# Expert outputs weighted at the PSUM eviction and accumulated into the residual in DRAM by the scatter

## What is computed

```
h2 = rmsnorm(x, g_ffn)
# top-1 of 4 groups, then top-2 of the 8 experts in it: 2 weights per token
for g in range(N_GROUPS):
    a = einsum('td,edf->tef', t, w_gate[g]); u = einsum('td,edf->tef', t, w_up[g])
    hid = silu(a) * u * combine[:, g, :, None]
    out = out + einsum('tef,efd->td', hid, w_down[g])
x = x + out
gate = sigmoid(rmsnorm(x, g_ple) @ w_ple_gate)
x = x + gate * (p @ w_ple_proj)
return rmsnorm(x, g_final)
```

## Time and profile before

| | us |
|---|---|
| median of 3 runs | 1550.75 (1549.37 to 1552.88) |
| the profiled execution | 1552.96 |
| its span on the slowest core, core 0 | 1551.4 |
| spans of the other seven cores | 1510.9 to 1547.7 |
| PE busy | 1103.8 (71%) |
| DVE busy | 733.3 (47%) |
| ACT busy | 727.7 (47%) |
| POOL busy | 491.0 (32%) |

### The profile page before, as it was taken

One profiled execution on the slowest core, in us unless ns is written; L12 is line 12 of the kernel. 1 busy time (PEld: TensorE's weight loads), 2 busy tenths in 40 slices (PEclk: granted clock), 3 DMA queues, 4 the chain that ended last, 5 costly groups with the idle time before them and its releaser, 6 DMA issues.

```text
span 1551.4 us, 24781 instructions; the slowest of 8 cores (1510.9 to 1551.4 us)
## 1 busy us (share of the span) xinstructions
PE 1103.8 (71%) x7772; PEld 716.7 (46%) x7772; DVE 733.3 (47%) x1283; ACT 727.7 (47%) x1376; POOL 491.0 (32%) x576
## 2 busy tenths in 40 slices
PE   2456389724972598870597999988989896852882
PEld 1123145413541354450475776766767674530341
DVE  4899877534752388437421222211212221116983
ACT  4888977625662488620142333332333332313652
POOL 3231132311221133130333433433434353111673
PEclk9767669856985598775698999999999998885986
DMA  9999995997699769935197898998788899568422
GB/s 224 217 142 136 110 106 89 139 135 102 84 136 136 107 90 132 167 129 189 29 237 180 214 219 208 220 241 226 185 227 200 224 162 167 148 214 306 163 109 110
DMA packets 74560, 254.32 MB, mean 164 GB/s; under 512 B 23735, under 2 KB 30647, under 8 KB 56000
## 3 DMA queue, kind: packets, MB, share of 16 engines
q0 software_dynamic: 43984, 134.60, 56.7%
q1 hardware_dynamic: 30448, 118.13, 23.0%
HBM read 434.85 MB, written 120.59 MB: 358 GB/s over the span
## 4 chain that ended last, share of the span: by engine, by line
PE 36%; DMA 26%; issue 12%; DVE 11%; ACT 6%; POOL 4%; another core or an unknown queue 4%; SPq 1%; DVEq 0%; ACTq 0%; POOLq 0%
PE ps L1377 14%; DMA sb_R<-h2scr,sb_R 7%; DMA sb_R<-xin 7%; PE ps L1349 7%; DMA xscr<-sb_R 3%; DMA sb_R<-w_pp 3%; PE ps L966 3%; DMA h2scr<-sb_R 2%; PE ps L1332 2%; PE ps L750 2%; DMA sb_R<-yscr 1%; DVE sb_R L1483 1%; POOL sb_R L1524 1%; PE ps L1003 1%
## 5 line engine op out<-in xcount | busy, mean ns | idle before, releaser
L1377 PE MATMUL ps<-sb_R 128*128 128x256 bf16 x3008 | 347.6, 277 | 6.2 <-DMA sb_R<-wall,sb_R 4.7
L1377 PEld LDWEIGHTS ps<-sb_R 128*128 128x128 bf16 x3008 | 298.7, 99 | 56.2 <-issue 7.1
L1382 DVE TENSOR_TENSOR sb_R<-sb_R,ps 128x512 bf16<-128x512 f32 x94 | 64.6, 688 | 317.7 <-PE ps L1377 269.1
L1359 POOL DMA_INDIRECT yscr<-sb_R x94 | 94.6, 1007 | 337.7 <-DVE sb_R L1356 296.8
L1349 PE MATMUL ps<-sb_R 128*128 128x512 bf16 x752 | 178.2, 390 | 0.8
L1381 ACT ACTIVATE sb_R<-ps 128x512 f32<-128x512 f32 x94 | 56.1, 597 | 258.1 <-PE ps L1377 209.5
L1335 ACT COPY sb_R<-ps 128x1024 bf16<-128x1024 bf16 x94 | 95.2, 1012 | 133.7 <-PE ps L1332 130.0
L1356 DVE COPY sb_R<-ps 128x512 f32<-128x512 f32 x94 | 64.9, 691 | 175.6 <-ACT sb_R L1354 89.7
L1303 POOL DMA_INDIRECT sb_R<-h2scr,sb_R x94 | 97.4, 1036 | 91.0 <-DVE sb_R L1262 62.2
L1349 PEld LDWEIGHTS ps<-sb_R 128*128 128x128 bf16 x752 | 73.0, 100 | 85.7 <-issue 13.9
L840 PE MATMUL ps<-sb_R 128*128 128x512 bf16 x128 | 36.3, 434 | 72.9 <-ACT sb_R L996 71.0
(11 more groups left out here) (248 smaller groups left out, 2098.1 us busy)
## 6 DMA issues: line engine op xcount, KB each, us to landing
wbf<-wall POOLq DMA_DIRECT2D x48, 1024.0 KB, 52.8
sb_R<-wbf SPq DMA_DIRECT2D x48, 1024.0 KB, 13.9
sb_R<-wall POOLq DMA_DIRECT2D x48, 1024.0 KB, 17.0
...
```

Of the source, the lines that this page charges most:

```text
L1359: return e.indirect_dma_start(y_d, bass.IndirectOffsetOnAxis(ap=didx[:, blk:blk + 1], axis=0), y.ap, None, bounds_check=breg(e, 2 * T_OWN ...
L1377: ins = e.matmul(pv[:, q * N:(q + 1) * N], lhsT=w_[:, c, f * P:(f + 1) * P], rhs=hT_[:, c, 0:N], start=(c == 0), stop=(c == 7))
```

## The change

Each expert output is scaled by its token's routing weight when it is evicted from PSUM, and the scatter adds it to the token's row of `xscr`, the residual, in DRAM. `yscr`, its loads in the tail and the two DVE operations per tile are gone. The one-hot matmuls now bring per slot the token number (from a new constant table `tokv`) and the weight `wsl`; the index of the second output place is not needed. These one-hot tiles are f32 instead of bf16.

Since two scatters may add to the same row, each scatter is given waits: with n scatters recorded before it and h the half of its block pair, `after=Yd[max(0, n - 2 - h):]`, which always includes the one just before. The first one also waits for all writes of `xscr`. In the tail the loads of x now wait for all scatters.

```diff
+ACC_FROM = lambda n, h: max(0, n - 2 - h)
...
-    y_d = dt("yscr", [2 * T_OWN, D], F32, kind="Internal").ap()
...
+        OHr = [a.rearrange("p t e -> p (t e)").rearrange("p (j n) -> p j n", j=4) for a in (gef, Ssl)]
+        OHq = [R.alloc(8 * NB).rearrange("p (j n) -> p j n", j=4) for _ in range(2)]
...
-            S.op("dve", lambda e, z=z: e.tensor_scalar(OHq[z][:, :, 0:NB], OHm[z], pc1, None, ALU.mult),
+            S.op("dve", lambda e, z=z, lo=lo: e.tensor_tensor(OHq[z][:, :, 0:NB], OHm[z], bg(tokv[:, lo:lo + 4], NB), ALU.mult),
                  reads=[OHm_b[z], cst_b], writes=[OH_b[z]])
-            S.op("dve", lambda e, z=z, lo=lo: e.tensor_tensor(OHq[z][:, :, NB:2 * NB], OHm[z], bg(iota[:, lo:lo + 4], NB), ALU.mult),
+            S.op("dve", lambda e, z=z, lo=lo: e.tensor_tensor(OHq[z][:, :, NB:2 * NB], OHm[z], bg(w12[:, lo:lo + 4], NB), ALU.mult),
...
-        dv(lambda e: e.tensor_copy(iT, p5[:, NB:2 * NB]), extra=[p5])
...
-        dv(lambda e: e.tensor_copy(iTi, iT))
-        dv(lambda e: e.tensor_scalar(iTi, iTi, 1, None, ALU.arith_shift_right))
-        dv(lambda e: e.tensor_copy(dsf, iTi))
-        dv(lambda e: e.scalar_tensor_tensor(dsf, dsf, float(P), inv, ALU.mult, ALU.add))
-        S.op("dve", lambda e: e.tensor_copy(gidx, dsf), reads=[rtb], writes=[ix_b])
-        dv(lambda e: e.scalar_tensor_tensor(dsf, iT, float(P), inv, ALU.mult, ALU.add))
-        S.op("dve", lambda e: e.tensor_copy(didx, dsf), reads=[rtb, ix_b], writes=[ix_b])
+        S.op("dve", lambda e: e.tensor_copy(gidx, inv), reads=[rtb], writes=[ix_b])
+        S.op("dve", lambda e: e.tensor_copy(wsl, p5[:, NB:2 * NB]), reads=[p5], writes=[ws_b])
...
-                        S.op("act", lambda e, y=y, pd=pd: e.copy(y[:, 0:512], pd.ap), reads=[pd], writes=[y])
+                        S.op("act", lambda e, y=y, pd=pd, blk=blk: e.activation(y[:, 0:512], pd.ap, AF.Copy, scale=wsl[:, blk:blk + 1]),
+                             reads=[pd, ws_b], writes=[y])
                     else:
-                        S.op("dve", lambda e, y=y, pd=pd: e.tensor_copy(y[:, 512:1024], pd.ap), reads=[pd], writes=[y])
+                        S.op("dve", lambda e, y=y, pd=pd, blk=blk: e.tensor_scalar(y[:, 512:1024], pd.ap, wsl[:, blk:blk + 1], None, ALU.mult),
+                             reads=[pd, ws_b], writes=[y])
...
-                    return e.indirect_dma_start(y_d, bass.IndirectOffsetOnAxis(ap=didx[:, blk:blk + 1], axis=0),
-                                                y.ap, None, bounds_check=breg(e, 2 * T_OWN - 1), oob_is_err=False)
+                    return e.indirect_dma_start(xs_d, bass.IndirectOffsetOnAxis(ap=gidx[:, blk:blk + 1], axis=0),
+                                                y.ap, None, bounds_check=breg(e, T_OWN - 1), oob_is_err=False, compute_op=ALU.add)
                 yb = B(f"Yd{blk}")
+                S.dmaop("pool", fn, reads=[y, ix_b] + (Xd if not Yd else []), writes=[yb], sembuf=y, after=Yd[ACC_FROM(len(Yd), h):], kb=512)
                 Yd.append(yb)
-                S.dmaop("pool", fn, reads=[y, ix_b], writes=[yb], sembuf=y, kb=512)
...
-                S.dmaop("sp", lambda e, x=x, ot=ot: e.dma_start(out=x.ap, in_=xs_d[ot * P:(ot + 1) * P, :]), reads=[Xd[ot]], writes=[x], kb=512)
-                S.dmaop("sp", lambda e, yt=yt, ot=ot: e.dma_start(out=yt.ap.rearrange("p (k d) -> p k d", k=2),
-                                                                 in_=y_d[ot * 2 * P:(ot + 1) * 2 * P, :].rearrange("(k p) d -> p k d", k=2)),
-                        reads=Yd, writes=[yt], kb=1024)
-                for k, wk in ((0, w1), (1, w2)):
-                    S.op("dve", lambda e, ot=ot, k=k, wk=wk, yt=yt, x=x: e.scalar_tensor_tensor(
-                        x.ap, yt[:, k * D:(k + 1) * D], wk[:, ot:ot + 1], x.ap, ALU.mult, ALU.add),
-                        reads=[yt, cw_b, x], writes=[x])
+                S.dmaop("sp", lambda e, x=x, ot=ot: e.dma_start(out=x.ap, in_=xs_d[ot * P:(ot + 1) * P, :]), reads=[Xd[ot]] + Yd, writes=[x], kb=512)
```

More of the change, by code:

```diff
@@ L589, in build @@
     wall_d = dt("wall", [NE, P, 12288], F32, kind="ExternalInput").ap()
-    cst_d = dt("cst", [P, 2 * P + 1], F32, kind="ExternalInput").ap()
+    cst_d = dt("cst", [P, 2 * P + 33], F32, kind="ExternalInput").ap()
     wbf_d = dt("wbf", [NE, P, 12288], BF16, kind="Internal").ap()
@@ L632, in build @@
         ix_b = B("ix"); ox_b = B("ox"); cw_b = B("cw"); cst_b = B("cst")
-        gidx = R.alloc(NB, I32, ix_b); didx = R.alloc(NB, I32, ix_b); oidx = R.alloc(NOVF, I32, ox_b)
-        w1 = R.alloc(NT, F32, cw_b); w2 = R.alloc(NT, F32, cw_b)
-        cst = R.alloc(2 * P + 1, F32, cst_b)
+        gidx = R.alloc(NB, I32, ix_b); ws_b = B("ws"); wsl = R.alloc(NB, F32, ws_b); oidx = R.alloc(NOVF, I32, ox_b)
+        w12 = R.alloc(2 * NT, F32, cw_b); w1 = w12.rearrange("p (t k) -> p t k", k=2)[:, :, 0]; w2 = w12.rearrange("p (t k) -> p t k", k=2)[:, :, 1]
+        cst = R.alloc(2 * P + 33, F32, cst_b)
+        tokv = cst[:, 2 * P + 1:2 * P + 33]
         iota = cst[:, 0:P]; utri32 = cst[:, P:2 * P]; pc1 = cst[:, 2 * P:2 * P + 1]
@@ L1136, in build @@
         slots3 = slots.rearrange("p (t k) -> p t k", t=NT)
-        OHr = [R.alloc(4 * P, BF16).rearrange("p (j n) -> p j n", j=4) for _ in range(2)]
-        OHq = [R.alloc(8 * NB, BF16).rearrange("p (j n) -> p j n", j=4) for _ in range(2)]
+        OHr = [a.rearrange("p t e -> p (t e)").rearrange("p (j n) -> p j n", j=4) for a in (gef, Ssl)]
+        OHq = [R.alloc(8 * NB).rearrange("p (j n) -> p j n", j=4) for _ in range(2)]
         OHm1 = R.alloc(4 * NB).rearrange("p (j n) -> p j n", j=4); OHm = [OHm1, OHm1]; OHm1_b = B("OHm"); OHm_b = [OHm1_b, OHm1_b]
         OH_b = [B(f"OH{i}") for i in range(4)]; OHr_b = [B(f"OHr{i}") for i in range(4)]
-        p1T = R.alloc(NB); iT = R.alloc(NB); inv = R.alloc(NB); dsf = R.alloc(NB); iTi = R.alloc(NB, I32)
+        p1T = R.alloc(NB); inv = R.alloc(NB)
         rtb.ranges.append((disp_off, R.off)); rtb.older = None
@@ L1238, in build @@
                  reads=[qr_b, cst_b], writes=[OHm_b[z]])
[L1239 removed]
+            S.op("dve", lambda e, z=z, lo=lo: e.tensor_tensor(OHq[z][:, :, 0:NB], OHm[z], bg(tokv[:, lo:lo + 4], NB), ALU.mult),
                  reads=[OHm_b[z], cst_b], writes=[OH_b[z]])
[L1241 to L1242 removed]
+            S.op("dve", lambda e, z=z, lo=lo: e.tensor_tensor(OHq[z][:, :, NB:2 * NB], OHm[z], bg(w12[:, lo:lo + 4], NB), ALU.mult),
+                 reads=[OHm_b[z], cw_b], writes=[OH_b[z]])
             def mmi(e, g=g, z=z):
@@ L1440, in build @@
         R.off = off0
-        TY = R.pool(S, "ty", 2048, 3)
         tx_off = R.off; R.off += 10240
@@ L1551, in make_in_maps @@
     cst = np.ascontiguousarray(np.concatenate([np.broadcast_to(ar[None, :], (P, P)),
-                                               (ar[:, None] < ar[None, :]).astype(np.float32), ar[:, None] + 1.0], axis=1))
+                                               (ar[:, None] < ar[None, :]).astype(np.float32), ar[:, None] + 1.0,
+                                               (np.arange(2 * NT) // 2 * P).astype(np.float32)[None, :] + ar[:, None] + 1.0], axis=1))
     w_pg = f(inp["w_ple_gate"])[0]; w_pp = f(inp["w_ple_proj"])[0]
```

3 lines of the change are left out of this document (1 added, 2 removed).

## The result

| | before | after |
|---|---|---|
| median, us | 1551.82 (1549.37 to 1555.83) | 1786.68 (1767.6 to 1806.21) |
| the profiled execution | 1552.96 | 1779.88 |
| its span on the slowest core | 1551.4 (core 0) | 1778.3 (core 1) |
| DVE busy | 733.3 | 691.5 |
| PE busy | 1103.8 | 1152.4 |

The change makes the kernel slower: a ratio of 1.147, with a 95% interval of 1.1361 to 1.1578. It saves what it removes, 17 MB of traffic and 42 us of DVE, and loses 227 us of span. The forecast was 1733 us with a range of 1635 to 1875. Some executions are slowed on one half of the chip; medians and ranges are over all executions, ratios and their intervals over the undisturbed ones alone, so a ratio can differ from that of two medians.

A forecast was written before the change was run, and what follows sets the result against it. PE bounds the kernel; the waits would put POOL's chain of landings ahead of it. Rounds +165, start +10, end +40, dispatch +4, tail -37 sum to +182 on 1553: 1735 profiled, 1733 us median, range 1635 to 1875.

The forecast's parts named there:

- The landing behind wall loads: Expert rounds: the even expert's first scatter lands behind wall loads and overflow gathers, 31.5 us after the first wall load.
- rival 1: Expert stage: POOL's slack absorbs the waits, leaving tail and dispatch, 1520 us; needs landings behind wall loads under 14; chance 0.09.
- The near-empty scatter: Second halves and overflow blocks: one landing, issue to semaphore, takes 3.1 us, bounds 2.2 and 3.75.
- The full one: Full accumulating scatter: one landing takes 5.4 us, the data time doubled for the add; bounds 4.2 and 8.5.
- Rival 2: Expert stage: the add itself is slow, a full scatter costs 8 us more, twice a round, 1940 us; chance 0.09.
- The 1.5 us set aside for sharing: Expert rounds: SP's three loads share the engines with wall loads, 1.5 us a round (0 to 7), making it 53.
- Start of the stage: Start of the expert stage: the first scatters stand behind two wall loads, +10 us (5 to 15).
- End of the stage: Last wall loads: transfers run dry while POOL walks scatters and gathers between sets, four gaps of 10, +40 us (20 to 70).
- The evictions: Expert stage: evictions by weight on ACT and DVE cost the same as before and are hidden anyway.
- The dispatch: Just ahead of the expert stage: fewer DVE operations, -2.5, and f32 one-hot matmuls, +6.5; together +4 us (-2 to +40).
- The tail: After the last scatter: yscr loads and DVE adds gone, xscr loads wait for the last scatter; -37 us (-22 to -57).
- 3, half absorbed: Expert stage: PE loses only half of the 15 us a round, 1651 us; counted inside the forecast's range, at its low end.

The follow-up runs named there:

- e1: The kernel before with only the waits added, each plain scatter to yscr waiting for the one just before: 1709.67 us, ratio 1.0986.
- e2: The kernel after, waits kept, its scatter overwriting instead of adding, so the residual and one of a token's two outputs are lost: 1687.27 us, ratio 1.0843.

## Why the prediction was right

**What bounds the kernel.** Right: PE before, POOL's chain of landings after, with PE waiting for what POOL issues late. Three of the signs that were named came, the second a little short: the scatter's own transfer as main releaser, with 348.0 us (over 300 was said); single waits of up to 25.9 us behind each set of wall loads (25 to 32 was said); sets 55.5 us apart (50 to 56). The idle time of PE in the stage rose by 198.6 us, where about 200 were said: PE was busy 565.5 of 650 us from 750 to 1400 before and 616.9 of 900 from 750 to 1650 after, 84.5 us idle against 283.1. It was to rise at the transposes alone; of the 220 us that PE now waits for POOL's late transfers, 78 are at the weights of overflow experts, which the prediction didn't name.

**The landing behind wall loads** was the step with most weight, read from a near-empty gather in the earlier trace rows: 31.5 us after the first load, measured 32.0 with its successor's wake-up. It decided against rival 1, which needed less than 14.

**The near-empty scatter**, 3.1, took 2.8 (the chain at 914.97) to 4.9 (at 909.26); its interval was 3.6 in the mean. **The full one**, 5.4, was sized too low: 7.15 in the chain at 980.90, an interval of 7.9, though within the bounds of 4.2 and 8.5. Rival 2 needed over 10. Two parts were missing. The plain one already takes 5.1 to 5.4 as an interval (e1, e2) where I had 4.2, as nothing had been put down for the wake-up of POOL, 0.8 us from that landing, 980.90 + 7.15, to the next issue at 988.84; and the add cost more than a second 1.14 us: 7.9 - 5.4 = 2.5, of which up to 0.6 can be POOL's longer issue.

**POOL's issue** wasn't thought of: I took 1.0 to 1.33 us for each, and an accumulating scatter takes 1.6. Nor was the last scatter of a round: its successor goes out 6.4 us after the wall load in the mean, where the issues ahead of it alone make 5.2, since it is issued just ahead of three wall loads and took 7.82 us (chain, 875.02) instead of 3.1. The round was 4.0 us over the 51.5 of the steps: 1.9 in the full scatter, 1.2 from the even expert's second scatter to the first overflow one (the issue time and a wait for an eviction, as the 1.48 us at 914.97), 0.5 in the stretch of overflow load and gathers, 0.5 up to the landing behind the wall loads. The 1.5 us set aside for sharing took up a part of that by luck, which left 2.5.

**Start of the stage**, +10 (5 to 15), measured +19, outside its own bounds. The cause named was right, its size had no sum behind it: the first scatter, behind two wall loads, had an interval of 18.5 us (789.14 to 807.62 on POOL; 1.3 before) and the next full one 7.6, and of these 23.4 us more POOL's slack before the first set took up about 5. **End of the stage**, +40, measured +39, in part by luck. From the first load after the twelfth set to the last one it took 113.5 us instead of 67.5 (1581.07 - 1467.62 and 1310.73 - 1243.23), five gaps that grew by 46 together where four of 10 were said; 5.5 came ahead of them, and the way from the last load to the last landing became 12.3 shorter, which no term had.

**The evictions** were put at no cost. By line, after (answer to the earlier trace rows):

```profile
L1352 DVE TENSOR_SCALAR sb_R<-ps,sb_R 128x512 f32<-128x512 f32 x94 | 70.6, 751 | 333.5 <-PE ps L1344 256.3 <-ACT sb_R L1349 77.1
L1349 ACT ACTIVATE sb_R<-ps,sb_R 128x512 f32<-128x512 f32 x94 | 65.0, 691 | 55.4 <-PE ps L1344 55.2
```

Wrong by a size that costs nothing: 751 ns against 691, and 691 against 588. L1381, from which the price was read, has no scale by a column. ACT and DVE, busy 73 and 45 of the 300 us from 900 to 1200, hide the 15.6 us in all.

**The dispatch** was put at +4. The one-hot matmuls, after (answer to the earlier trace rows):

```profile
L1248 PE MATMUL ps<-sb_R 128*128 128x188 f32 x64 | 19.6, 486 | 25.7 <-DVE sb_R L1242 25.7
```

Busy 19.6 us, where 32 x 0.7 = 22.4 had been assumed; before it was 6.3. The count doubled, each f32 matmul standing in the records as two. The first gather came 7.3 us later on the slowest core, of which an unknown part is from before the dispatch: on core 0 it was 2.1 (756.81 against 754.74).

**The tail**, -37, measured -31. The first rstd, in place of the earlier trace rows, on POOL (start, us):

```profile
1641.48 1.54 POOL L1356 DMA_INDIRECT xscr<-sb_R  x1 [6.00 <-DMA xscr<-sb_R]
1655.35 0.19 POOL L716 TENSOR_SCALAR sb_R<-sb_R 128x4 f32<-128x4 f32 x1 [12.32 <-ACT sb_R L1475]
```

It started 1655.35 - 1646.3 = 9.05 us behind the last landing (10 to 12 was said), against 30.7 before: -21.7 where -20 was said. What follows gave -9 instead of -17. DVE lost 42 us in all: 46.4 of adds are gone, and the evictions took back 5.7.

**Rivals.** 1 was wrong by its own point of decision. 2 was wrong on size, but its direction showed: the add is worth 97 us in the chain. In the forecast it carried far less: by its own bound, with a free add two landings a round would be 1.14 us shorter. 3, half absorbed, didn't show: PE's idle time grew by 198.6 us and the stage by 250.7. The rest is PE itself, whose matmuls took longer while it was granted less: a clock of 0.83 in the mean from 900 to 1200 us, where it was 0.98 before. Its two costliest groups, after (columns as in the earlier trace rows):

```profile
L1374 PE MATMUL ps<-sb_R 128*128 128x256 bf16 x3008 | 368.2, 286 | 79.1 <-DMA sb_R<-wall,sb_R 77.6 <-ACT sb_R L1330 1.5
L1344 PE MATMUL ps<-sb_R 128*128 128x512 bf16 x752 | 192.1, 411 | 5.5 <-ACT sb_R L1349 2.0 <-DVE sb_R L1352 1.6 <-ACT sb_R L1330 0.8
```

Before they were busy 347.6 and 178.2 us, 34.5 less together, for the same matmuls. With 13.3 us of f32 one-hot matmuls that makes 47.8 of the 48.6 us by which PE's busy time grew; smaller groups moved both ways. It isn't a cost of its own, as POOL is the bound.

So the mechanism and the place were right, and the sum was 45 us short: 27 in the rounds, for the most part the full scatter's price (11 x 1.9 = 21), 9 at the start by the landing behind two wall loads, 6 in the tail and 3 ahead of the stage.
